# Convolved channels projected by a seven-product block form, two channels at a time, in a hybrid DeltaNet, attention and MoE block on one Trainium2 core

## The reference

```python
p = h @ w_in                                   # h: (1, 2048, 1024)
qkv_a = p[..., :1536]
qkv_a = silu(causal_dwconv(qkv_a, w_conv))     # 4 taps, each column on its own
qa, ka = l2norm(q heads) * 128**-0.5, l2norm(k heads)
oa = gated_delta_rule(qa, ka, va, beta, g)     # chunks of tokens, in sequence
...
x += gate * (concat(oa, ob) @ w_out)           # ob: dilated window attention
x += gate * hierarchical_moe(rmsnorm(x) ...)   # top-2 of 32 experts
return rmsnorm(x)
```

## Time and profile before

| | before |
|---|---|
| runs, median (three) | 2424.84 us |
| the profiled execution, its span | 2421.4 us |
| TensorE busy | 2199.4 us (91%) |
| VectorE / ScalarE / GpSimd busy | 1117.7 / 916.9 / 387.2 us |
| convolved channels 0 to 11 on TensorE | 296.2 to 628.5 us |
| channel 12 | 628.5 to 656.0 us |

### The profile page before, as it was taken

One profiled execution on the slowest core, in us unless ns is written; L12 is line 12 of the kernel. 1 busy time (PEld: TensorE's weight loads), 2 busy tenths in 40 slices (PEclk: granted clock), 3 DMA queues, 4 the chain that ended last, 5 costly groups with the idle time before them and its releaser, 6 DMA issues. The chain is left out here.

```text
span 2421.4 us, 33277 instructions
## 1 busy us (share of the span) xinstructions
PE 2199.4 (91%) x9996; PEld 1238.2 (51%) x9997; DVE 1117.7 (46%) x2278; ACT 916.9 (38%) x2135; POOL 387.2 (16%) x320
## 2 busy tenths in 40 slices
PE   5999999999999998897999998999948998999980
PEld 2666544444455545886777775555533333333330
DVE  4444232223244761454888876678652222222223
ACT  1333121111133321223779874434314443444433
POOL 0000000000011100345333210010121222222220
PEclk9999999999999998898999999999968999999995
DMA  8444112311255644986233324545465888889737
GB/s 342 147 148 157 68 40 79 122 52 61 100 159 182 204 164 139 301 274 212 94 97 106 102 92 131 182 149 158 138 230 162 290 279 290 292 273 311 208 78 295
DMA packets 178321, 418.15 MB, mean 173 GB/s; under 512 B 41192, under 2 KB 81000, under 8 KB 162744
## 3 DMA queue, kind: packets, MB, share of 16 engines
q1 hardware_dynamic: 155944, 346.59, 41.3%
q0 software_dynamic: 13472, 45.26, 8.1%
q10 hardware_dynamic: 8816, 25.18, 3.0%
HBM read 296.84 MB, written 124.85 MB: 174 GB/s over the span
## 5 line engine op out<-in xcount | busy, mean ns | idle before, releaser
L2168 PE MATMUL ps<-big,bias 128*64 x672 | 302.1, 603 | 2.7 <-DVE ex_wgu L2260 1.8
L2169 PE MATMUL ps<-ex_wgu,bias 128*64 128x512 f32 x672 | 302.1, 603 | 0.0
L693 PE MATMUL ps<-big,w_chan 128*128 128x512 f32 x640 | 277.3, 592 | 3.2 <-PEq L139 3.2
L693 PE MATMUL ps<-big,pc_w 128*128 128x512 f32 x640 | 277.5, 592 | 0.0
L1686 PE MATMUL ps<-w_out,mo_yt 128*128 128x512 f32 x512 | 226.4, 600 | 0.0
L345 PE MATMUL ps<-cp_wt,big 128*128 128x344 f32 x768 | 225.1, 453 | 0.0
L693 PEld LDWEIGHTS ps<-big,w_chan 128*128 128x128 f32 x640 | 121.5, 190 | 153.2 <-issue 152.8
L693 PEld LDWEIGHTS ps<-big,pc_w 128*128 128x128 f32 x640 | 121.4, 190 | 149.3 <-issue 148.9
L345 PEld LDWEIGHTS ps<-cp_wt,big 128*128 128x128 f32 x768 | 145.7, 191 | 76.8 <-issue 3.8
L1418 PE MATMUL ps<-at_v,at_pt 128*128 128x128 f32 (+1 forms) x1200 | 182.8, 290 | 0.0
L2168 PEld LDWEIGHTS ps<-big,bias 128*64 128x64 f32 x672 | 89.7, 138 | 181.6 <-issue 181.6
(11 more groups left out here) (315 smaller groups left out, 3303.1 us busy)
## 6 DMA issues: line engine op xcount, KB each, us to landing
big<-in_w_gate_up SPq DMA_DIRECT2D x32, 2048.0 KB, 9.9
w_out<-in_w_down SPq DMA_DIRECT2D x32, 1024.0 KB, 5.4
cp_w<-in_w_ada SPq DMA_DIRECT2D x24, 1024.0 KB, 5.2
ch_d<-pc_cv SPq DMA_DIRECT2D x20, 1024.0 KB, 4.2
at_v<-v_d SPq DMA_DIRECT2D x27, 512.0 KB, 3.9
o_d<-at_o SPq DMA_DIRECT2D x48, 264.0 KB, 2.1
mo<-o_d SPq DMA_DIRECT2D x16, 792.0 KB
pc_qkv<-ch_d SPq DMA_DIRECT2D x16, 768.0 KB, 5.5
```

What stands on the lines that cost most here:

```text
L693: last = nc.tensor.matmul(ps[:, n % 2, :], w[ch % 2][:, k, :], m.ht[:, k, g * BANK:(g + 1) * BANK], start=(k == 0), stop=(k == KD - 1))
L2168: nc.tensor.matmul(ps[0:HB, 2 + b, :], xt[:, b, k, 0:HB], wgu[:, bass.ds(at * WGU + k * 2 * DE, 2 * DE)], start=(k == 0), stop=(k == KD - 1))
L2169: last = nc.tensor.matmul(ps[HB:P, 2 + b, :], xt[:, b, k, HB:P], wgu2[:, b, k, :], start=(k == 0), stop=(k == KD - 1))
```

## The change

The twelve convolved channels are taken as six pairs, and the tokens as two halves of 1024: twelve steps, each one pair by one half ("quad"), pairs running inside halves. In a quad the feature axis is cut in two (A's columns, B's rows: `KH` = 4 blocks of 128), the two channels are the rows of A, and the two groups of 512 tokens are the columns of B. The 2x2 block product, eight half-products of 4 matmuls each before, is done with seven (Winograd's form of Strassen's scheme): with S2 = A21 + A22 - A11 and so on for weights, T1 to T4 for tokens.

- GpSimd makes the mixed weights S1 to S4 of each quad (`mixed_weights`, four instructions of 128x512) and T3 of each half (`mixed_tokens`, 128x2048); VectorE makes T1, T2, T4 of each half (three of 128x2048).
- TensorE runs seven products of four matmuls (`quad`) in banks 0 and 1; three of them add to a bank that has been read in between.
- ScalarE reads a bank twice a quad (`take_quad`), VectorE five times with an addition (`add_up`), into `p1`, `u2`, `u3` and `pre`.
- The convolution works on 1024 tokens of a channel (`conv(s, c)`); the last three columns of a half are kept for the next in `hist`. Each is placed between the additions of the next quad.
- SyncE loads two channels' weights a quad (`load_pair`), each pair twice in all, into `w_chan`, `pc_w` and a part of `mod`. Other tiles are laid over one another to make room. GpSimd clears its two tiles after the last quad.

```diff
+                def load_pair(s):
+                    if s >= 2:
+                        sp.wait_ge(*ch_done.n(STEPS_Q * (s - 1)))
+                    for c in range(2):
+                        if s or c:
+                            sp.dma_start(wp[s % 2][c], a["w_chan"][2 * (s % PAIRS) + c]).then_inc(*wp_in[s % 2].inc)
...
-                load_w(1)
+                load_pair(0)
+                load_pair(1)
                 sp.dma_start(al[:, :], row_bc(a["a_log"], GH)).then_inc(*small_in.inc)
...
+                def mixed_tokens(s):
+                    if s:
+                        pool.wait_ge(*ch_done.n(STEPS_Q * (s - 1) + 4))
+                    nc.gpsimd.tensor_tensor(tb[:, 2, :, :], m.ht[:, KH:, tokens(s, 1)], m.ht[:, 0:KH, tokens(s, 1)], ALU.subtract).then_inc(*t3_ready.inc)
+
+                def mixed_weights(s):
+                    one, two = wp[s % 2]
+                    pool.wait_ge(*wp_in[s % 2].n(2 * (s // 2) + 1 + s % 2))
+                    if s >= 2:
+                        pool.wait_ge(*ch_done.n(STEPS_Q * (s - 1)))
+                    s2, s3, s4 = (sw[:, s % 2, j, :, :] for j in range(3))
+                    nc.gpsimd.tensor_tensor(s3, one[:, 0:KH, :], two[:, 0:KH, :], ALU.subtract)
+                    link(nc.gpsimd.tensor_tensor(two[:, 0:KH, :], two[:, 0:KH, :], two[:, KH:, :], ALU.add))
+                    link(nc.gpsimd.tensor_tensor(s2, two[:, 0:KH, :], one[:, 0:KH, :], ALU.subtract))
+                    nc.gpsimd.tensor_tensor(s4, one[:, KH:, :], s2, ALU.subtract).then_inc(*s_ready.inc)
...
+                def product(bank, lhs, rhs, fresh):
+                    for k in range(KH):
+                        last = nc.tensor.matmul(ps[:, bank, :], lhs[:, k, :], rhs[:, k, :], start=(fresh and k == 0), stop=(k == KH - 1), skip_group_check=(not fresh))
+                    last.then_inc(*ch_done.inc)
...
+                    if s:
+                        pe.wait_ge(*wp_in[s % 2].n(2 * (s // 2) + 1 + s % 2))
+                        pe.wait_ge(*sum_read.n(READS_D * s - 1))
+                    product(b0, a11, b11, True)
+                    pe.wait_ge(*s_ready.n(s + 1))
+                    pe.wait_ge(*t_ready.n(3 * half + 2))
+                    if s:
+                        pe.wait_ge(*sum_read.n(READS_D * s))
+                    product(b1, s2, t2, True)
+                    pe.wait_ge(*ch_read.n(READS_A * s + 1))
+                    product(b0, a12, b21, False)
+                    pe.wait_ge(*t3_ready.n(half + 1))
+                    pe.wait_ge(*sum_read.n(READS_D * s + 1))
+                    product(b1, s3, t3, True)
+                    pe.wait_ge(*ch_read.n(READS_A * s + 2))
+                    product(b0, s1, t1, True)
+                    pe.wait_ge(*t_ready.n(3 * half + 3))
+                    pe.wait_ge(*sum_read.n(READS_D * s + 2))
+                    product(b1, a22, t4, False)
+                    pe.wait_ge(*sum_read.n(READS_D * s + 3))
+                    product(b0, s4, b22, False)
...
-                for n in range(GROUPS):
-                    group(n)
+                quad(0)
                 sums()
...
+                for s in range(1, NCONV):
+                    quad(s)
+                for n in range(NCONV * GROUPS, AHEAD):
                     group(n)
...
+                    nc.scalar.copy(p1[:, :], ps[:, b, :]).then_inc(*ch_read.inc)
+                    act.wait_ge(*ch_done.n(STEPS_Q * s + 3))
+                    if s >= 2:
+                        act.wait_ge(*cv_ready.n(s - 1))
+                    nc.scalar.copy(pre[:, b, 0, HIST:HIST + BANK], ps[:, b, :]).then_inc(*ch_read.inc)
...
+                def add_up(s, n, to, to_add, bank, step):
+
+                    dve.wait_ge(*ch_done.n(STEPS_Q * s + step))
+                    if n == 0:
+                        dve.wait_ge(*ch_read.n(READS_A * s + 1))
+                    else:
+                        dve.wait_ge(*sum_read.n(READS_D * s + n))
+                    V.tensor_tensor(to, to_add, ps[:, bank, :], ALU.add).then_inc(*sum_read.inc)
+
+                for s in range(NCONV + 1):
+                    b = s % 2
+                    if s:
+                        conv(s - 1, 0)
+                    if s < NCONV:
+                        add_up(s, 0, u2[:, :], p1[:, :], 1 - b, 2)
...
+                    if s:
+                        conv(s - 1, 1)
...
+                    add_up(s, 1, u3[:, :], u2[:, :], 1 - b, 4)
...
+                    add_up(s, 2, pre[:, b, 1, HIST + BANK:], u3[:, :], b, 5)
...
+                    add_up(s, 3, pre[:, b, 1, HIST:HIST + BANK], u2[:, :], 1 - b, 6)
...
+                    add_up(s, 4, pre[:, b, 0, HIST + BANK:], u2[:, :], b, 7)
```

More of the change, by code:

```diff
@@ L537, in project_channels, with tokens, group_done, group_read @@
         REST = groups_at(NT + 2)[-1] + 1
+        def tokens(s, second):
+            at = s // PAIRS * HT + second * BANK
+            return slice(at, at + BANK)
+        def group_done(n):
+            return DONE0 + n - NCONV * GROUPS + 1
+        def group_read(n):
+            return READ0 + n - NCONV * GROUPS + 1
         scores = ps[:, KKQ:KKQ + 2, :].rearrange("p k (a x n) -> p (k a) x n", a=2, x=2)
@@ L685, in _, with quad @@
             def _(pe):
+                def product(bank, lhs, rhs, fresh):
+                    for k in range(KH):
+                        last = nc.tensor.matmul(ps[:, bank, :], lhs[:, k, :], rhs[:, k, :], start=(fresh and k == 0), stop=(k == KH - 1), skip_group_check=(not fresh))
+                    last.then_inc(*ch_done.inc)
+                def quad(s):
+                    b0, b1 = s % 2, 1 - s % 2
+                    one, two = wp[s % 2]
+                    a11, a12, s1, a22 = one[:, 0:KH, :], one[:, KH:, :], two[:, 0:KH, :], two[:, KH:, :]
+                    s2, s3, s4 = (sw[:, s % 2, j, :, :] for j in range(3))
+                    b11, b21, b22 = m.ht[:, 0:KH, tokens(s, 0)], m.ht[:, KH:, tokens(s, 0)], m.ht[:, KH:, tokens(s, 1)]
+                    t1, t2, t3, t4 = (tb[:, j, :, :] for j in range(4))
+                    half = s // PAIRS
+                    if s:
[19 more added lines that the diff above has]
+                    product(b0, s4, b22, False)
@@ L816, in _ @@
                 act.wait_ge(*zeroed.n(2))
-                for n in range(GROUPS + 2):
-                    take_group(n)
+                take_quad(0)
                 act.wait_ge(*diff_ready.n(1))
@@ L865, in _ @@
-                conv(0)
-                dve.wait_ge(*sums_done.n(1))
-                link(V.tensor_copy(m.gsum[:, :], ps[:, SUM, 0:NT * GH]))
-                V.tensor_tensor(m.kdec[:, :], last, m.gsum[:, :], ALU.subtract).then_inc(*diff_ready.inc)
-                dve.wait_ge(*bias_done.n(1))
-                for n in range(NB):
-                    V.tensor_tensor(row[:, n, :], ps[0:AH, ROWS + n, 0:BIAS_W], off[:, n, :], ALU.add).then_inc(*row_ready.inc)
-                conv(1)
-                dve.wait_ge(*eg_ready.n(1))
@@ L874, in _, with conv @@
-                V.scalar_tensor_tensor(m.nbe[:, :], m.beta[:, :], -1.0, t[:, 2, :, :].rearrange("p t n -> p (t n)"), ALU.mult, ALU.mult).then_inc(*nbe_ready.inc)
-                for ch in range(2, NCONV):
-                    conv(ch)
+                def conv(s, c):
+                    b, half = s % 2, s // PAIRS
+                    ch = 2 * (s % PAIRS) + c
+                    if c == 0:
+                        dve.wait_ge(*ch_read.n(READS_A * (s + 1)))
+                        dve.wait_ge(*sum_read.n(READS_D * (s + 1)))
+                        dve.wait_ge(*cv_out[b].n(s // 2))
+                        both = slice(ch, ch + 2)
+                        if half == 0:
+                            V.tensor_copy(hist[:, both, :], pre[:, b, :, HT:HT + HIST]).then_inc(*hist_ready.inc)
+                        else:
+                            V.tensor_copy(pre[:, b, :, 0:HIST], hist[:, both, :]).then_inc(*hist_ready.inc)
+                        dve.wait_ge(*hist_ready.n(s + 1))
+                    to = cv[:, b, c * HT:(c + 1) * HT]
+                    link(V.tensor_scalar(to, pre[:, b, c, 0:HT], wc[:, ch * CONV:ch * CONV + 1], None, ALU.mult))
+                    for n in range(1, CONV):
+                        ins = V.scalar_tensor_tensor(to, pre[:, b, c, n:n + HT], wc[:, ch * CONV + n:ch * CONV + n + 1], to, ALU.mult, ALU.add)
+                        if n < CONV - 1 or c == 0:
+                            link(ins)
+                    if c:
+                        ins.then_inc(*cv_ready.inc)
```

169 lines of the change are left out of this document (115 added, 54 removed).

## The result

The changed kernel takes 2395.73 us (median of 4 runs, 2393.01 to 2396.49), the one before 2422.81 on the same chip (4 runs, 2420.14 to 2427.37): ratio 0.9889, 95% interval 0.9868 to 0.991. It is 27 to 29 us faster; the forecast was 2396.4, a gain of 28.4 from a median of 2424.84.

What follows compares the result with a forecast made beforehand. The convolution stage was taken as bound by TensorE alone, at full clock without gaps. Saving 41.2 less 10.2 (first wait), 2.0 (clock) and 0.6 (GpSimd beside VectorE) gives 28.4: 2424.84 to 2396.4 us, range 2388 to 2406.

Steps and rivals of the forecast that it cites:

- Removed: Convolved channels on TensorE: 336 matmuls in place of 384, 48 fewer at 0.858 us, 41.2 us saved.
- The rival in which every start costs 0.2 us: Each of 84 product starts on TensorE pays 0.2 us, 17 in all: 2413 us; chance 0.09 for 0.2 or less.
- The first wait and the clock: First quad: TensorE stands 10.2 us before product 1, then loses 2.0 us at the lower clock.
- the term of 10.2: First quad: TensorE stands 10.2 us between products 0 and 1, awaiting mixed weights; bounds 8.5 and 15.
- the 9 to 11 that I had named as the sign: Sign of being right: one TensorE gap of 9 to 11 us behind product 0, with GpSimd as releaser.
- The longer first wait: First quad: GpSimd's arithmetic falls later or the load lands later, 6 us more, 2402 us; chance 0.15.
- the one with loading of GpSimd's code: First quad: about 6 us for GpSimd's first call, paid behind the load, 2402 us; no separate chance given.
- Product 2 needs ScalarE's copy of product 0 ... Nothing there waits: First quad: ScalarE, free at 309.1 before, is ready some 2 us later, 311, still within product 1; no wait.
- Ports: GpSimd beside VectorE: some VectorE instructions wait for GpSimd; cost 0.6 us, up to 2.5 in quads 5 and 6.
- my worst case: In each quad, all GpSimd time in reach adds to VectorE's: second add ends at 15.6 us, before 17.2.
- The rival in which VectorE becomes the bound: GpSimd and VectorE hamper each other, product 5 starts 3.4 us late, eleven quads lose 37 us: 2433; chance 0.05.
- Costed at nothing: Doubled weight traffic, history copies, late memsets and the other order of the stage's end: no cost.

Runs made afterwards that it cites:

- prefetch: Changed kernel with the second channel's weights also loaded in the stage ahead: 2393.54 us, 0.9858 to 0.9914 of the kernel before.
- prefetch_order: Changed kernel with second channel's weights loaded a stage ahead, small loads earlier, ScalarE's first copy, VectorE's first addition and T4 ahead of the decay gates: 2385.69 us.
- conv_plus: Changed kernel with three more VectorE `tensor_scalar` of 1024 elements per quad ahead of the second convolution: 2409.43 us, 0.9925 to 0.9964 of the kernel before.

## Why the prediction was right

**Removed, 41.2 us: shown.** 672 instructions, 24.03 us a quad, no price on a product's start. The rival in which every start costs 0.2 us falls: products start 3.43 us apart (361.34 to 364.77), eight times 0.429.

**The first wait and the clock, 12.2 us forecast, 11.7 measured**: from the stage's start to product 2 are 18.57 us (298.95 to 317.52), where two products take 6.87. Product 1 started 13.3 us after the stage's start (forecast 13.7: the load was issued at 4.2, not 4.3, landed within 3.9, not 4.0, and the mixes took 5.1, not 5.3). Less a product of 3.43, that is 9.9 us for the term of 10.2. The row itself shows an idle time of 8.03 us, under the 9 to 11 that I had named as the sign, because product 0 ran at the lower clock for a while and ended 1.7 us late; that lay inside the wait for S2 and cost nothing. The clock behind the gap took 1.85 us in product 1, where 2.0 was taken. I had excluded a loss at the 3.22 us gap, from one row; of twelve profiles with that same gap six lost some 1.6 us behind it. What decides it no run shows. The longer first wait falls (the landing was 3.9 us), and so does the one with loading of GpSimd's code: its first instruction of the stage took 1.26 us, with the data, at 307.03. The Trainium skill's figure of about 6 us for a first call ("GPSIMD Engine Reference", section 2.1 Instruction dispatch) is not seen here, where GpSimd had 8 us of waiting in which it would be hidden; prefetch, where the first mix starts at once, has 3.34 us, which VectorE's instruction explains.

**The step that failed: "Product 2 needs ScalarE's copy of product 0 ... Nothing there waits".** In the changed kernel it was right in one profile, by the luck of 0.03 us, and wrong in the other: 3.46 us. Five of seven profiles that have a mixed first quad show this wait (2.44 to 5.26 us); the sixth, prefetch_order, had the copy moved, and the seventh is the first profile of the changed kernel. Two things were wrong in it. The small loads were put "some 2 us later"; VectorE's instruction that waits for them starts 13.2 us after the stage's start, and 8.2 before (304.41), so 5.0 later: its last load was issued 1.3 us later, and came 6.65 us after that, in place of 3.0. That alone brought it to where T3 begins (the mixes end at 312.2), and left the copy 0.8 us of room where I had counted on more than two. And I had counted ScalarE's own time behind the small loads, and not that what it waits for, a 0.23 us instruction on VectorE, can be held by GpSimd's longest one. Where the wait comes, the stage gains 24.5 us (332.29 less 307.78) and not 28.2. How often it comes in the timed runs isn't known: the totals don't show it, as start and rest scatter by more. That the first median met the forecast within 0.7 us, and the first profile the stage's 28.4 within 0.2, is in part luck.

**Ports.** The steady quads have no stall, as forecast, but less room than I gave them. In quad 5 of the changed kernel the second sum ends at 449.31, and product 5 is due at 450.60 (433.44 and five products): 1.3 us, under the 1.6 of my worst case, in which all of GpSimd's time was added. In quad 6 the block of VectorE costs 1.07 + 0.24 and another 0.07, 1.4 us, where 0.6 was taken and 2.5 was the bound. VectorE's timeline of quad 5, in which it makes that sum and then mixes the second half's tokens, beside GpSimd's T3:

```profile
448.63 0.68 DVE L1016 TENSOR_TENSOR pc_u<-pc_u,ps 128x512 f32<-128x512 f32 x1
...
449.80 4.53 POOL L722 TENSOR_TENSOR pc_chunk<-big 128x2048 f32<-128x2048 f32 x1
...
451.41 5.06 DVE L964 TENSOR_TENSOR pc_chunk<-big 128x2048 f32<-128x2048 f32 x1
```

and in quad 6, where a sum that reads PSUM is not held and the convolution is:

```profile
466.16 1.88 POOL L730 TENSOR_TENSOR pc_qkv<-mod 128x512 f32<-128x512 f32 x1 [11.83 <-DMA mod<-in_w_chan]
...
466.94 0.69 DVE L1016 TENSOR_TENSOR pc_u<-pc_p,ps 128x512 f32<-128x512 f32 x1
467.55 1.04 DVE L1001 TENSOR_SCALAR pc_cv<-pc_pre,pc_wc 128x1024 f32<-128x1024 f32 x1
468.62 2.17 DVE L1003 SCALAR_TENSOR_TENSOR pc_cv<-pc_pre,pc_wc,pc_cv 128x1024 f32<-128x1024 f32 x1
```

L964 takes 2.29 us alone; GpSimd's instruction ends at 454.33, 2.9 us after it began, and the rest of its 5.06 us, 2.1, is about its own work. That is an exclusive hold for a whole instruction, in both directions: GpSimd's mixes of 1.26 us last 3.3 beside a 2.29 us instruction. The rule of the Trainium skill that the prediction weighed ("SBUF — State Buffer", section "SBUF: two separate sides") holds in kind and size, and I should have used it at the stage's start too, where it prices the small instruction at GpSimd's 4.5 us. The rival in which VectorE becomes the bound falls by the changed kernel, which stalls only in quad 6, and by conv_plus: 2.25 us more work cost 0.56 in six quads and about 2 in quads 4 and 5, so there it is not far off.

**Costed at nothing.** The end of the stage is as it was: the load of the first chunk is issued 20.4 us after channel 12 starts and first used at 42.9 (before: 20.3 and 42.9).

## What to carry to other kernels

A block form that saves TensorE an eighth is worth its eighth where TensorE is without gaps, if the adds and mixes fit beside it; take its fill at the front from the plain form, whose first operands are there. When a step "has slack" on one engine, follow what that engine waits for through every queue, down to the smallest instruction, and ask which long GpSimd instruction it can fall behind. When two rows that can hold each other start 0.03 us apart, one profile shows one of two outcomes, and only a second profile tells the other.

## What the runs showed of the hardware

- VectorE and GpSimd hold each other for whole instructions: 0.23 us became 4.51 to 4.57 behind a 4.50 us GpSimd instruction (four profiles), 1.26 on GpSimd became 3.3 beside 2.29 on VectorE. Instructions of VectorE that read PSUM kept their 0.69 us.
- Taking a wait away can cost much of what it gives: with the data there at once (prefetch), two of GpSimd's four mixes moved beside VectorE's and each grew by 2 us.
- A small load issued behind three loads of 512 KB was used 6.65 us after its issue (changed kernel), and 3.0 us behind one such load (before: 301.40 to 304.41).
- A gap of 3.22 us on TensorE was followed by the lower clock (0.50 of 2.4 GHz, 1.2 GHz) for some 3 us in six of twelve profiles; later gaps of 3.99 to 9.51 us were each followed by a slow product (5.4 to 6.7 us in place of 3.6), and gaps of 2.59 and 3.44 to 3.56 us by one of 3.70. In conv_plus a gap of 2.44 us, right behind a slow product, had a slow one behind it too (5.40).
- A stall of TensorE costs about 0.24 us more than its idle time (24.59 us less 24.03 and 0.32, conv_plus). As much stands before each weight load; that it is the same time isn't shown.
